# One stage for output projection, first norm and expert layer in a hybrid decoder step

## The chip, the core and the metric

The kernel runs on one core of one Trainium2 chip. The metric is the device time of one execution in microseconds (us); smaller is better. The core has a matrix engine (TensorE, PE in the profile), a vector engine (VectorE, DVE), an activation engine (ScalarE, ACT), a general engine (GpSimd, POOL) and a queue engine (SyncE, SP) that only issues DMAs here. Each engine runs its own list of instructions in order; they meet through semaphores. Three runs of the kernel before gave 3161.84, 3165.94 and 3166.44 us, the median is 3165.94 us.

## The reference, cut to what matters

One decoder layer is computed for 272 prompt positions (16 meta tokens and 256 tokens) and 32 sample positions, width 2048, all in float32. After an input projection and two mixers (a recurrent one and a sparse attention), the part that the change touches is:

```
def finish_layer(x, y_rwkv, y_attn, w_o, ln1_g, ln1_b, peer_wq, peer_subkeys, peer_u, peer_v, ln2_g, ln2_b):
    mix = jnp.concatenate([y_rwkv, y_attn], axis=-1) @ w_o
    x = layer_norm(DN_ALPHA * x + mix, ln1_g, ln1_b)
    return layer_norm(DN_ALPHA * x + peer_ffn(x, peer_wq, peer_subkeys, peer_u, peer_v), ln2_g, ln2_b)
```

`peer_ffn` projects each position to 16 query halves (`x @ peer_wq`), scores them against keys, picks 16 experts of 16384 for each of 8 heads, and sums `gate * gelu(x . u_expert) * v_expert`. The meta positions are dropped after the mixers, so 288 positions remain (256 prompt, 32 sample).

## The kernel before, in words

`build` (line 346) calls a row of phases through `Ctx.phase` (line 114). A phase is one block of code in which all engines run side by side; all engines meet at its end, SP clears the phase's semaphores in a small block of its own, and the next phase starts. So nothing of a later phase, loads included, begins before the phase in front of it is done.

Activations lie transposed: 128 partitions are 128 of the 2048 features, `KT` = 16 blocks of features follow in the free dimension, and positions are innermost. A weight tile is 128 x 2048 floats (1 MB). Products that need more than the reduced `fp32r` precision are split: ACT rounds a tile to `fp32r` ("high"), DVE subtracts ("low"), and `split_product` (line 269) makes three matmuls on lines 272 to 274: high by high, high by low, low by high. A tile is therefore loaded by SP, raised by ACT, lowered by DVE, and then used by PE in 48 matmuls.

After the mixers, five phases follow on lines 385 to 396:

1. `load` "rest" (line 388): the residual, 2.25 MB, from a DRAM buffer into `x_midT`.
2. `split` "mix" (lines 251 to 266): the mixers' output `mixT` into high and low, in four quarters, ACT (line 258) and then DVE (line 264).
3. `project` "out" (line 277): 16 tiles of `w_o`. SP loads four tiles ahead (line 306), ACT raises into two buffers (line 314), DVE lowers the next tile (line 332) ahead of evacuating this one (line 392: `alpha * x + product` into `x_midT`). PE runs 48 matmuls of 288 columns for each tile.
4. `layer_norm` "ln1" (line 179): the mean over features is 16 full-precision matmuls by a matrix of 1/2048 (line 199, two records each), DVE copies and subtracts it in four quarters (lines 210 and 212), ACT squares (line 231), PE sums the squares (line 203), DVE adds epsilon and takes the reciprocal (lines 215 and 216), ACT takes the root (line 234), DVE multiplies 16 blocks by gain and root (line 220) and adds the shift in 16 more (line 224), into `mixT`.
5. `peer_layer` (line 1931): the expert layer, one phase with an order written out by hand. The list `order` puts a query tile of `peer_wq` before every second expert tile as long as there are queries (16), then 128 tiles of `peer_u` ("up", line 2201 and after) and 128 tiles of `peer_v` ("down"). Four weight slots (`SL` = 4) turn in that order: SP loads the next tile of the list once PE is done with the one four places before (line 2073 and after). At the start of the phase, ACT and DVE split the normed activations into `high` and `low` (lines 2286 and 2485), DVE spreads the sample columns (line 2480), PE makes the first query (line 2178: 16 full-precision matmuls of two records each), turns the sample columns (line 2160), and then runs `up(0)`.

The rest of `peer_layer` goes by the number of the tile: `select` on DVE picks the experts in tiles 4 to 35, POOL sends 256 scatters of gates to DRAM (line 2122) as heads are chosen, and gathers the sample rows by indirect DMAs (line 2142); DVE multiplies these in certain tiles (line 2439). DVE's list has these steps between the lowering of tiles (line 2327), so a wait for a gathered row holds up the tile behind it.

Of the kernel before, what the change touches and what calls it, by code (L numbers as in the profile page):

```python
# [19 lines left out]
P = 128  # L20
D = 2048
# [324 lines left out]
def build(nc, a, o):  # L346

    cx = Ctx(nc)
    with ExitStack() as top:
# [35 lines left out]
        with ExitStack() as late:  # L385

            xT = sb("x_midT", [P, KT, NY], stack=late)
            cx.phase(load, "rest", ((xT[:], x_rest[:, :, META:N]),))
            high, low = sb("mix_high", [P, KT, NY], F32R, late), sb("mix_low", [P, KT, NY], F32R, late)
            cx.phase(split, "mix", mixT[:, :, META:N], high, low)  # L390
            cx.phase(project, "out", KT, a["w_o"], high, low,
                    lambda v, c, acc: v.scalar_tensor_tensor(xT[:, c, :], xT[:, c, :], ALPHA, acc,
                                                             ALU.mult, ALU.add))
# [1531 lines left out]
def peer(cx, a, o, xT, whole, ident, gates_d):  # L1925


    cx.phase(peer_layer, a, o, xT, whole, ident, gates_d)


def peer_layer(cx, a, o, xT, whole, ident, gates_d):
# [15 lines left out]
    order = []  # L1947
# [22 lines left out]
    with ExitStack() as st:  # L1970
# [5 lines left out]
        parts = nc.alloc_sbuf_tensor_at("px_parts", [P, S, D], F32, offset=begin)  # L1976
        rows = sb("rows", [P, 2, D])
        xs, acc_s = sb("xs", [P, D]), sb("acc_s", [P, D])
# [3 lines left out]
        fetch = [sb(f"fetch{s}", [P, D]) for s in range(UG)]  # L1982
# [29 lines left out]
        here = begin  # L2012

# [7 lines left out]

        hid = [again(f"hid{s}", [P, NP]) for s in range(HS)]
# [8 lines left out]
        loaded = [cx.sem(f"px_loaded{s}") for s in range(SL)]  # L2031
        keyed = [cx.sem(f"px_keyed{s}") for s in range(4)]
# [18 lines left out]
        with nc.Block() as block:  # L2051
            @block.sync
            def _(sp):
# [18 lines left out]
                for kind, n in order:  # L2072
                    s, turn = slot(kind, n)
                    if turn:
                        before, m = order[at[kind, n] - SL]
                        sp.wait_ge(projected if before == "query" else multiplied, m + 1)
# [35 lines left out]
            def _(pool):  # L2112
                sent = 0
# [37 lines left out]
                pool.wait_ge(multiplied, NK)  # L2151
# [3 lines left out]
            def _(pe):  # L2155
# [15 lines left out]

                def query(c):
# [4 lines left out]
                    for k in range(KT):  # L2177
# [69 lines left out]
            def _(act):  # L2247
                def prepare(u):
                    s, turn = slot("tile", u)
                    act.wait_ge(loaded[s], 16 * (turn + 1))  # L2250
                    if u >= WH:
                        act.wait_ge(multiplied, u - WH + 1)
# [418 lines left out]
```

## Time and profile before

| | us |
|---|---|
| median of 3 runs (3161.84 to 3166.44) | 3165.94 |
| the profiled execution's own time | 3163.14 |
| its span, first to last instruction | 3161.5 |
| PE busy | 2820.4 (89%) |
| DVE busy | 1805.1 (57%) |
| ACT busy | 986.4 (31%) |
| POOL busy | 772.3 (24%) |
| mean granted clock of TensorE | 0.932 |

Rows of a timeline give the start from the span's beginning, the duration, the engine, the line of the code, the operation, and what it writes and reads; `x4` means that four of the kind follow each other and are shown as one, and brackets at the end give the engine's idle time before the row and what ended it. Rows of a table of stretches give busy time and number of instructions of PE, PEld (weight loads), DVE, ACT and POOL in that order, then the granted clock of TensorE as a share of its full 2.4 GHz, the busy share of the DMA engines and GB/s.

### The profile page before, as it was taken

The page shows a single profiled execution, that of the slowest core. Times are in us where ns is not written, and L with a number is a line of the kernel's source. Part 1 is how long each engine was busy: PE and PEld are TensorE (multiplying, and loading weights), DVE is VectorE, ACT ScalarE, POOL GpSimd, SP SyncE. Part 2 cuts the span into 40 slices and gives each one's busy share as a digit, 9 for nine tenths or more (in the row PEclk, how much of TensorE's full clock was granted, in tenths as well). Part 3 has the DMA queues.
Part 4 walks back from the last instruction along what each step waited for, and adds up shares of the span by engine and source line. Part 5 has one row for each costly group of instructions (what it writes and reads, how often), then busy time and mean ns, then how long its engine had stood idle before and what let it go on. Part 6 is the DMA issues. An engine that isn't in the chain of part 4 may idle for free.

```text
span 3161.5 us, 45193 instructions
## 1 busy us (share of the span) xinstructions
PE 2820.4 (89%) x17548; PEld 2427.2 (77%) x17548; DVE 1805.1 (57%) x2598; ACT 986.4 (31%) x1169; POOL 772.3 (24%) x630
## 2 busy tenths in 40 slices
PE   3999984767988999759699997999999999999997
PEld 2999972456666666549599997999999888888886
DVE  3455541198774443233468895555656667666655
ACT  1454530011221111122323233333334434434343
POOL 0100002210000222200018787888840000000000
PEclk7999997687889999879899998999999999999999
DMA  3355434322223555242356666999888888876664
GB/s 124 134 185 182 160 142 126 95 68 63 62 67 107 162 154 155 77 145 105 124 166 173 177 180 173 295 300 289 296 309 304 327 303 306 308 275 249 246 237 176
DMA packets 245312, 594.93 MB, mean 188 GB/s; under 512 B 76345, under 2 KB 180162, under 8 KB 192658
## 3 DMA queue, kind: packets, MB, share of 16 engines
q1 hardware_dynamic: 173874, 484.95, 44.8%
q0 software_dynamic: 54592, 90.41, 10.7%
q10 hardware_dynamic: 16640, 16.78, 1.6%
q8 instruction: 135, 2.21, 0.3%
q14 instruction: 71, 0.58, 0.1%
HBM read 535.05 MB, written 56.97 MB: 187 GB/s over the span
## 4 chain that ended last, share of the span: by engine, by line
PE 31%; POOL 12%; issue 5%; DMA 3%; DVE 1%; ACT 0%; DVEq 0%; POOLq 0%
POOL expert_gates L2122 12%; PE px_bank L272 10%; PE px_bank L274 10%; PE px_bank L273 10%; PE px_bank L2178 1%; DMA expert_gates<-px_chosen,px_spot 1%; POOL px_fetch L2142 1%; DMA px_w<-in_peer_v 1%; DMA px_parts<-sample_parts 0%; DMA px_fetch<-in_peer_rows,px_spots_s 0%; ACT px_wh L2253 0%; DMA px_w<-in_peer_wq 0%; DVE px_rows L2514 0%; DMA px_w<-in_peer_u 0%; DVE px_fetch L2519 0%
## 5 line engine op out<-in xcount | busy, mean ns | idle before, releaser
L2327 DVE TENSOR_TENSOR px_w_r<-px_w,px_wh 128x2048 fp32r<-128x2048 f32 x256 | 585.8, 2291 | 278.9 <-ACT px_wh L2253 278.5
L2253 ACT ACTIVATE px_wh<-px_w 128x2048 fp32r<-128x2048 f32 x256 | 489.8, 1913 | 593.1 <-PE px_bank L274 242.3
L272 PE MATMUL px_bank<-px_high,px_wh 128*128 128x256 f32 x2048 | 584.5, 285 | 24.2 <-DVE px_w_r L2327 24.2
L2122 POOL DMA_INDIRECT expert_gates<-px_chosen,px_spot x256 | 499.0, 1949 | 430.3 <-DVE px_chosen L2401 322.9
L273 PE MATMUL px_bank<-px_low,px_wh 128*128 128x256 f32 x2048 | 581.4, 284 | 0.0
L274 PE MATMUL px_bank<-px_high,px_w_r 128*128 128x256 f32 x2048 | 581.4, 284 | 0.0
L272 PEld LDWEIGHTS px_bank<-px_high,px_wh 128*128 128x128 f32 x2048 | 395.2, 193 | 25.6 <-DVE px_w_r L2327 25.6
L272 PE MATMUL px_bank<-px_wh,px_gh 128*128 128x512 f32 x1024 | 398.5, 389 | 1.2 <-DVE px_gl L2333 1.2
L274 PE MATMUL px_bank<-px_wh,px_gl 128*128 128x512 f32 x1024 | 398.4, 389 | 0.0
L273 PE MATMUL px_bank<-px_w_r,px_gh 128*128 128x512 f32 x1024 | 398.4, 389 | 0.0
L273 PEld LDWEIGHTS px_bank<-px_low,px_wh 128*128 128x128 f32 x2048 | 395.2, 193 | 0.0
L274 PEld LDWEIGHTS px_bank<-px_high,px_w_r 128*128 128x128 f32 x2048 | 395.0, 193 | 0.0
L272 PE MATMUL pj_acc<-mixT_r,pj_wh 128*128 128x304 f32 x784 | 244.4, 312 | 44.0 <-DVE pj_w_r L630 44.0
L274 PE MATMUL pj_acc<-mixT_r,pj_w_r 128*128 128x304 f32 x784 | 241.3, 308 | 0.0
L273 PE MATMUL pj_acc<-x_inT_r,pj_wh 128*128 128x304 f32 x784 | 239.4, 305 | 0.0
L272 PEld LDWEIGHTS px_bank<-px_wh,px_gh 128*128 128x128 f32 x1024 | 192.2, 188 | 41.8 <-DVE px_w_r L2327 1.1
L273 PEld LDWEIGHTS px_bank<-px_w_r,px_gh 128*128 128x128 f32 x1024 | 192.2, 188 | 40.0
L274 PEld LDWEIGHTS px_bank<-px_wh,px_gl 128*128 128x128 f32 x1024 | 192.2, 188 | 39.9
L630 DVE TENSOR_TENSOR pj_w_r<-pj_w,pj_wh 128x2048 fp32r<-128x2048 f32 x49 | 112.7, 2302 | 184.0 <-ACT pj_wh L531 184.0
L272 PEld LDWEIGHTS pj_acc<-mixT_r,pj_wh 128*128 128x128 f32 x784 | 149.9, 191 | 48.6 <-DVE pj_w_r L630 44.7
L2439 DVE SCALAR_TENSOR_TENSOR px_fetch<-px_fetch,px_xs 128x2048 f32<-128x2048 f32 x32 | 73.4, 2292 | 142.2 <-DMA px_fetch<-in_peer_rows,px_spots_s 142.2
L2274 ACT ACTIVATE px_h<-px_bank 128x256 f32<-128x256 f32 x128 | 48.8, 382 | 329.2 <-PE px_bank L274 325.5
(392 smaller groups left out, 4352.1 us busy)
## 6 DMA issues: line engine op xcount, KB each, us to landing
px_w<-in_peer_u SPq DMA_DIRECT2D x128, 1024.0 KB, 5.4
px_w<-in_peer_v SPq DMA_DIRECT2D x128, 1024.0 KB, 4.9
pj_w<-in_w_in SPq DMA_DIRECT2D x49, 1024.0 KB, 4.9
expert_gates<-rh_empty ACTq DMA_DIRECT2D x16, 1024.0 KB, 6.4
at_values<-in_kv_pages POOLq DMA_DIRECT2D x128, 128.0 KB, 2.7
at_pages<-in_kv_pages SPq DMA_DIRECT2D x128, 128.0 KB, 2.2
out_w<-in_w_o SPq DMA_DIRECT2D x16, 1024.0 KB, 4.8
px_w<-in_peer_wq SPq DMA_DIRECT2D x16, 1024.0 KB, 4.9
```

Source lines behind the costliest of these rows:

```text
L272: pe.matmul(out, w_high, high, start=start, stop=False, skip_group_check=True)
L273: pe.matmul(out, w_high, low, start=False, stop=False, skip_group_check=True)
L274: return pe.matmul(out, w_low, high, start=False, stop=stop, skip_group_check=True)
L630: v.tensor_tensor(w_low[c % SL][:], w[c % SL][:], w_high[c % 2][:], ALU.subtract).then_inc(lowered, 1)
L2122: pool.indirect_dma_start(gates_d, bass.IndirectOffsetOnAxis(ap=spot[:, t, z:z + 1], axis=0), chosen[:, 2, t, z:z + 1], None, compute_op=A ...
L2142: pool.indirect_dma_start(fetch[n % UG][:], None, a["peer_rows"] if n < TS else a["peer_v"], bass.IndirectOffsetOnAxis(ap=spots_s[:, r:r + ...
L2178: mm = pe.matmul(acc[:, 0:NY], w[s][:, k * P:k * P + P], xT[:, k, :], start=k == 0, stop=k == KT - 1)
L2253: act.activation(w_high[u % WH][:], w[s][:], ACT.Copy).then_inc(raised, 1)
L2274: act.activation(h[i % HS][:], bank[i % 4][:, 0:NP], ACT.Gelu).then_inc(curved, 1)
L2327: v.tensor_tensor(w_low[s][:], w[s][:], w_high[u % WH][:], ALU.subtract).then_inc(lowered, 1)
L2439: v.scalar_tensor_tensor(to[:], to[:], 1.0, xs[:], ALU.mult, ALU.mult, accum_out=dots[:, r:r + 1]).then_inc(dotted, 1)
```

## The change: what it does

The phases "rest", "mix", "out" and "ln1" are gone; their work moves to the front of `peer_layer`.

- **Weight stream.** The 16 tiles of `w_o` stand ahead of `order`, so they, the queries and the expert tiles pass through the same four slots. Three `w_high` buffers (`WH` = 3) are used where `project` had two. SP issues the first four tiles of `w_o`, then waits for the split of `mixT` (`m_split`) and loads the residual over `mixT`.
- **Split.** ACT raises the first weight tile, then the four quarters of `mixT`; DVE lowers the first quarter, the first weight tile, then the other quarters; PE starts a quarter of the first tile as each quarter is split.
- **Norm sums.** After tile 1, PE takes a rough mean from the first block alone (`first_mean`), DVE makes it a shift (`first_shift`). For every tile DVE evacuates (`empty`) and subtracts the shift (`move_y`), ACT squares the block (`square_y`), and POOL adds block and square to two running sums. After the last tile PE multiplies the two sums and the last block by the matrix of ones (`moments`, four matmuls in place of 32).
- **Rest of the norm.** `deviations` on DVE copies the mean, makes the variance as mean of squares less square of the mean, takes the reciprocal, and subtracts the mean from blocks 0 to 7 in two quarters; POOL subtracts it from blocks 8 to 15 in two quarters. ACT takes the root. DVE multiplies block by block, and ACT adds the shift block by block (`normed_x`).
- **Query 0** starts with block 0 of `normed_x` and takes each block as it comes.

The core of the diff:

```diff
-        with ExitStack() as late:
...
-            cx.phase(load, "rest", ((xT[:], x_rest[:, :, META:N]),))
...
-            cx.phase(split, "mix", mixT[:, :, META:N], high, low)
-            cx.phase(project, "out", KT, a["w_o"], high, low,
...
-            cx.phase(layer_norm, "ln1", xT, ln_gb[:, 1], ones, into=mixT[:, :, META:N])
-        peer(cx, a, o, mixT[:, :, META:N], mixT, ident, gates_d)
+        peer(cx, a, o, mixT[:, :, META:N], mixT, ident, gates_d, x_rest, ones, ln_gb[:, 1])
...
-    order = []
+    order = [("out", c) for c in range(KT)]
...
+                    if kind == "out":
+                        sp.dma_start(w[s][:].rearrange("p (k e) -> p k e", e=P), a["w_o"][n]).then_inc(loaded[s], 16)
+                        if n == 3:
+                            sp.wait_ge(m_split, 4)
+                            sp.dma_start(xT, x_rest[:, :, META:N]).then_inc(rest_in, 16)
+                        continue
...
             def _(pool):
+                for c in range(KT - 1):
+                    pool.wait_ge(moved_y, c + 1)
+                    if c:
+                        pool.wait_ge(summed_y, 2 * c)
+                    for to, x in ((sum_y, xT[:, c, :]), (sum_q, sq[c % 2][:])):
+                        if to is sum_q:
+                            pool.wait_ge(squared_y, c + 1)
+                        if c:
+                            pool.tensor_tensor(to[:], x, to[:], ALU.add).then_inc(summed_y, 1)
+                        else:
+                            pool.tensor_copy(to[:], x).then_inc(summed_y, 1)
+                pool.wait_ge(centered_x, 1)
...
+                for q_ in (2, 3):
+                    four = xT[:, 4 * q_:4 * q_ + 4, :]
+                    pool.tensor_tensor(four, four, norm[:, 1:2, :].to_broadcast([P, 4, NY]), ALU.subtract) \
+                        .then_inc(widened, 1)
...
+                def out(c):
+                    s, _ = slot("out", c)
+                    pe.wait_ge(lowered, c + 1)
+                    if c >= 4:
+                        pe.wait_ge(emptied, c - 3)
+                    for k in range(KT):
+                        if c == 0 and k % 4 == 0:
+                            pe.wait_ge(m_split, k // 4 + 1)
...
+                def first_mean():
+                    pe.wait_ge(emptied, 1)
+                    pe.matmul(bank[5][:, 0:NY], ones[:], xT[:, 0, :], start=True, stop=True).then_inc(shift_made, 1)
...
+                def moments():
+                    pe.wait_ge(summed_y, 2 * KT - 2)
+                    pe.wait_ge(shifted_by, 1)
+                    pe.matmul(bank[5][:, 0:NY], ones[:], sum_y[:], start=True, stop=False)
+                    pe.matmul(bank[6][:, 0:NY], ones[:], sum_q[:], start=True, stop=False)
+                    pe.wait_ge(moved_y, KT)
+                    pe.matmul(bank[5][:, 0:NY], ones[:], xT[:, KT - 1, :], start=False, stop=True).then_inc(meaned, 1)
+                    pe.wait_ge(squared_y, KT)
+                    pe.matmul(bank[6][:, 0:NY], ones[:], sq[(KT - 1) % 2][:], start=False, stop=True).then_inc(meaned, 1)
...
                     for k in range(KT):
+                        if c == 0:
+                            pe.wait_ge(normed_x, k + 1)
                         mm = pe.matmul(acc[:, 0:NY], w[s][:, k * P:k * P + P], xT[:, k, :], start=k == 0, stop=k == KT - 1)
...
+                for c in range(KT):
+                    out(c)
+                    if c == 1:
+                        first_mean()
+                moments()
...
+                prepare(-KT)
+                for z in range(4):
+                    act.activation(m_high[:, 4 * z:4 * z + 4, :], xT[:, 4 * z:4 * z + 4, :], ACT.Copy).then_inc(m_raised, 1)
+                act.activation(stat[:, 0, 7:8], ident[:, 0:1], ACT.Sqrt)
+                for c in range(KT):
+                    if c + 1 < KT:
+                        prepare(c + 1 - KT)
+                    if c:
+                        square_y(c - 1)
+                square_y(KT - 1)
+                act.wait_ge(deviated, 1)
+                act.activation(rs[:, 1, :], rs[:, 0, :], ACT.Sqrt).then_inc(deviated, 1)
+                for k in range(KT):
+                    act.wait_ge(scaled_x, k + 1)
+                    act.activation(xT[:, k, :], xT[:, k, :], ACT.Identity, bias=gb[:, 1, k:k + 1]).then_inc(normed_x, 1)
+                act.wait_ge(normed_x, KT)
...
+                def empty(c):
...
+                    if c == 0:
+                        v.wait_ge(rest_in, 16)
+                    v.scalar_tensor_tensor(x, x, ALPHA, bank[c % 4][:, 0:NY], ALU.mult, ALU.add).then_inc(emptied, 1)
+                def move_y(c):
...
+                    v.tensor_tensor(x, x, norm[:, 0, :], ALU.subtract).then_inc(moved_y, 1)
...
+                def deviations():
...
+                    v.wait_ge(meaned, 1)
+                    v.tensor_copy(norm[:, 1, :], bank[5][:, 0:NY]).then_inc(centered_x, 1)
+                    v.wait_ge(centered_x, 1)
+                    lk(v.tensor_tensor(norm[:, 2, :], norm[:, 1, :], norm[:, 1, :], ALU.mult))
+                    v.wait_ge(meaned, 2)
+                    lk(v.scalar_tensor_tensor(rs[:, 0, :], bank[6][:, 0:NY], LN_EPS, norm[:, 2, :], ALU.add, ALU.subtract))
+                    v.reciprocal(rs[:, 0, :], rs[:, 0, :]).then_inc(deviated, 1)
...
+                    for q_ in range(2):
+                        four = xT[:, 4 * q_:4 * q_ + 4, :]
+                        ins = v.tensor_tensor(four, four, norm[:, 1:2, :].to_broadcast([P, 4, NY]), ALU.subtract)
+                    lk(ins)
+                    v.wait_ge(deviated, 2)
+                    for k in range(KT):
+                        if k in (8, 12):
+                            v.wait_ge(widened, k // 4 - 1)
+                        v.scalar_tensor_tensor(xT[:, k, :], xT[:, k, :], gb[:, 0, k:k + 1], rs[:, 1, :],
+                                               ALU.mult, ALU.mult).then_inc(scaled_x, 1)
...
+                for z in range(4):
+                    v.wait_ge(m_raised, z + 1)
+                    v.tensor_tensor(m_low[:, 4 * z:4 * z + 4, :], xT[:, 4 * z:4 * z + 4, :],
+                                    m_high[:, 4 * z:4 * z + 4, :], ALU.subtract).then_inc(m_split, 1)
+                    if z == 0:
+                        prepare(-KT)
+                for c in range(KT):
+                    if c + 1 < KT:
+                        prepare(c + 1 - KT)
+                    empty(c)
+                    if c == 1:
+                        first_shift()
+                        move_y(0)
+                    if c:
+                        move_y(c)
+                deviations()
+                v.wait_ge(normed_x, KT)
```

In `out`, `square_y` and the lines left out, waits keep the buffers free of overlap; `prepare` on ACT now waits for PE to be three tiles behind. The new phase has 15 more semaphores than `peer_layer` had.

## Rows read from the trace of the kernel before

**Rows 1.** Table of stretches: output projection, norm to first expert matmul, first expert tiles.

```profile
1387.00:1491.60 104.60, 104.55 (x768) 104.31 (x768) 41.20 (x31) 26.85 (x15) 0.00 (x0) 0.98 0.36 130
1491.60:1549.04 57.44, 30.80 (x112) 23.19 (x113) 31.47 (x64) 13.84 (x14) 0.00 (x0) 0.76 0.22 78
1549.04:1642.00 92.96, 92.96 (x651) 86.23 (x650) 46.25 (x116) 28.88 (x35) 0.00 (x0) 1.00 0.49 170
```

**Rows 2.** Timeline, residual load to the first evacuation of the output projection, all engines.

```profile
1359.89 0.58 SPq L166 DMA_DIRECT2D x_midT<-x_rest  x1
...
1370.25 4.32 ACT L258 ACTIVATE mix_high<-mixT 128x1152 fp32r<-128x1152 f32 x4 [15.38 <-PEq L120]
1371.45 5.16 DVE L264 TENSOR_TENSOR mix_low<-mixT,mix_high 128x1152 fp32r<-128x1152 f32 x4 [15.05 <-ACT mix_high L258]
1377.77 88.69 SPq L306 DMA_DIRECT2D out_w<-in_w_o  x16
1382.72 1.91 ACT L314 ACTIVATE out_wh<-out_w 128x2048 fp32r<-128x2048 f32 x1 [8.14 <-DMA out_w<-in_w_o]
1384.66 4.69 DVE L332 TENSOR_TENSOR out_w_r<-out_w,out_wh 128x2048 fp32r<-128x2048 f32 x2 [8.05 <-ACT out_wh L314]
1387.01 0.61 PE L272 MATMUL out_acc<-mix_high,out_wh 128*128 128x288 f32 x1 [35.22 <-DVE out_w_r L332]
...
1395.72 0.45 DVE L392 SCALAR_TENSOR_TENSOR x_midT<-x_midT,out_acc 128x288 f32 x1 [6.38 <-PE out_acc L274]
```

**Rows 3.** Timeline, last evacuation to the first expert matmul, all engines.

```profile
1491.59 0.45 DVE L392 SCALAR_TENSOR_TENSOR x_midT<-x_midT,out_acc 128x288 f32<-128x288 f32 x1 [5.94 <-PE out_acc L274]
...
1506.51 9.72 PE L203 MATMUL ln_var<-ln_sq,ones 128*128 128x288 f32 x32 [3.14 <-ACT ln_sq L231]
...
1516.76 1.95 DVE L216 RECIPROCAL ln_rs<-ln_rs 128x288 f32<-128x288 f32 x1
...
1519.22 6.96 DVE L220 SCALAR_TENSOR_TENSOR x_midT<-x_midT,ln_gb,ln_rs 128x288 f32<-128x288 f32 x16 [0.51 <-ACT ln_rs L234]
...
1532.26 0.34 SPq L2078 DMA_DIRECT2D px_w<-in_peer_wq  x1
...
1532.52 2.19 DVE L2480 COPY px_acc_s<-mixT 128x128 f32<-128x128 f32 x16
...
1534.63 4.62 DVE L2485 TENSOR_TENSOR px_low<-mixT,px_high 128x1024 fp32r<-128x1024 f32 x4
...
1537.63 9.91 PE L2178 MATMUL px_bank<-mixT,px_w 128*128 128x288 f32 x32 [21.41 <-DMA px_w<-in_peer_wq]
...
1549.04 0.36 PE L272 MATMUL px_bank<-px_high,px_wh 128*128 128x256 f32 x1
```

**Rows 4.** The residual's tile: time from issue of its load to landing.

```profile
DMA to landing us min/median/max: 9.3/9.3/9.3
```

**Rows 5.** Chain of waits, second query (start, duration).

```profile
1561.22 7.76 PE px_bank L2178 x32
```

**Rows 6.** Table of stretches, the variance matmuls of the norm.

```profile
1506.50:1516.30 9.80, 9.72 (x32) 7.06 (x32) 2.60 (x4) 3.49 (x3) 0.00 (x0) 0.83 0.00 0
```

**Rows 7.** Timeline, elementwise work of POOL and DVE beside each other, in earlier phases.

```profile
86.27 4.94 DVE L630 TENSOR_TENSOR pj_w_r<-pj_w,pj_wh 128x2048 fp32r<-128x2048 f32 x2 [11.05 <-ACT pj_wh L531]
...
86.69 2.36 POOL L619 TENSOR_TENSOR pj_df<-pj_raw 128x272 f32<-128x272 f32 x1 [19.04 <-ACT pj_last L589]
...
98.72 0.64 POOL L619 TENSOR_TENSOR pj_df<-pj_raw 128x272 f32<-128x272 f32 x1 [7.26 <-ACT pj_last L589]
...
755.58 1.89 POOL L1110 TENSOR_TENSOR rh_bx<-rh_rows,rh_seqmask 128x1024 f32<-128x1024 f32 x1 [50.23 <-DMA rh_rows<-rw_rows]
...
755.86 1.77 DVE L1872 TENSOR_SCALAR at_prob<-at_prob,at_stat 128x272 f32<-128x272 f32 x1
...
806.47 0.50 DVE L1872 TENSOR_SCALAR at_prob<-at_prob,at_stat 128x272 f32<-128x272 f32 x1
```

**Rows 8.** Waits of PE from 1642 to 2165 us: total, times, longest.

```profile
PE px_bank L272 <- DVE px_w_r L2327: 24.2, 7, 12.6
```

More of the change, by code:

```diff
@@ L1976, in peer_layer @@
         parts = nc.alloc_sbuf_tensor_at("px_parts", [P, S, D], F32, offset=begin)
+        begin = -(-nc.sbuf_base // 32) * 32
         rows = sb("rows", [P, 2, D])
+        fetch = [sb(f"fetch{s}", [P, D]) for s in range(UG)]
+        m_high, m_low = (nc.alloc_sbuf_tensor_at(f"px_m_{x}", [P, KT, NY], F32R, offset=begin + z * KT * NY * 4)
+                         for z, x in enumerate(("high", "low")))
+        assert nc.sbuf_base >= begin + 2 * KT * NY * 4
         xs, acc_s = sb("xs", [P, D]), sb("acc_s", [P, D])
@@ L2012, in peer_layer @@
         here = begin
+        norm = sb("norm", [P, 3, NY])
         def again(name, shape, dt=F32):
@@ L2020, in again @@
             return t
+        here = begin + 4 * 4 * P
+        sq = [again(f"sq{s}", [P, NY]) for s in range(2)]
+        sum_y, sum_q = again("sum_y", [P, NY]), again("sum_q", [P, NY])
+        rs = again("rs", [P, 2, NY])
+        here = begin
         hid = [again(f"hid{s}", [P, NP]) for s in range(HS)]
@@ L2192, in up @@
                     s, _ = slot("tile", i)
-                    pe.wait_ge(lowered, i + 1)
+                    pe.wait_ge(lowered, KT + i + 1)
                     if i >= 4:
@@ L2206, in down @@
                     s, _ = slot("tile", u)
-                    pe.wait_ge(lowered, u + 1)
+                    pe.wait_ge(lowered, KT + u + 1)
                     pe.wait_ge(g_lowered, j + 1)
@@ L2248, in prepare @@
                 def prepare(u):
-                    s, turn = slot("tile", u)
+                    r = KT + u
+                    s, turn = slot("tile", u) if u >= 0 else slot("out", r)
                     act.wait_ge(loaded[s], 16 * (turn + 1))
-                    if u >= WH:
-                        act.wait_ge(multiplied, u - WH + 1)
-                    act.activation(w_high[u % WH][:], w[s][:], ACT.Copy).then_inc(raised, 1)
+                    if r >= WH:
+                        act.wait_ge(multiplied, r - WH + 1)
+                    act.activation(w_high[r % WH][:], w[s][:], ACT.Copy).then_inc(raised, 1)
                     if u >= NK:
@@ L2268, in keep_rows, with square_y @@
                     act.activation(rows[:, t, c * 512:c * 512 + 512], bank[7][:], ACT.Copy, scale=ALPHA).then_inc(rowed, 1)
+                def square_y(c):
+                    act.wait_ge(moved_y, c + 1)
+                    if c >= 2:
+                        act.wait_ge(summed_y, 2 * (c - 2) + 2)
+                    act.activation(sq[c % 2][:], xT[:, c, :], ACT.Square).then_inc(squared_y, 1)
                 def curve(i):
-                    act.wait_ge(multiplied, i + 1)
+                    act.wait_ge(multiplied, KT + i + 1)
                     if i >= HS:
@@ L2320, in prepare @@
                 def prepare(u):
-                    s, _ = slot("tile", u)
+                    r = KT + u
+                    s, _ = slot("tile", u) if u >= 0 else slot("out", r)
                     if u >= NK:
```

47 lines of the change are left out of this document (32 added, 15 removed).

## The prediction

> **What bounds the kernel now.** I read the table of stretches first. PE is busy for 104.55 of 104.60 us in the output projection and for all of 92.96 us once the expert tiles run; between them lie 57.44 us with 30.80 us of PE work at a granted clock of 0.76 [rows 1]. So the edges are open and the middle is not: PE sets the pace inside both product stages, and a serial chain through the other engines sets it in front of the first and between the two. The timelines of these edges come next. In front, the residual's load (1359.89), the split (1370.25), the first weight load (1377.77) and the first matmul (1387.01) follow each other [rows 2]. Between, the norm, a weight load (issued at 1532.26, its query at 1537.63) and the split stand in one line [rows 3]. Both are parts of the chain that I expect to set the end, since PE has no gap from 1549.04 to 1642 [rows 1] and what follows is numbered by tiles; the one later place where PE waits is 24.2 us in seven waits [rows 8].
>
> **The front.** The first DMA of the stage stays where the residual's was, at 1359.89, and is now a weight tile. In the old order the tile reached ACT 4.95 us after issue (1377.77 to 1382.72), and raising took 1.91 [rows 2]. So it is raised at 1366.75. Then ACT raises the first quarter of the mix (4.32 for four, 1.08 each) and DVE lowers it (5.16 for four, 1.29 each) [rows 2]: 1369.2. DVE then lowers the weight tile, 2.35, half of 4.69 [rows 2]; with hops 1371.7, and PE begins, against 1387.01 [rows 2]: **15.3 us gained**. The other quarters (1.29 each) finish before PE needs them, since a quarter of the first tile is over 2 us of PE: the first tile took 8.7 us (1387.01 to 1395.72) [rows 2].
>
> **The projection.** The other 15 tiles took 1395.72 to 1491.59, 6.39 each [rows 2, 3]. In the new list DVE does 2.35 + 0.45 + 0.46 (the move, taken as an evacuation) a tile, ACT 1.91 + 0.45 (the square, taken likewise), POOL two sums of 0.68 (0.64 for 272 columns, scaled to 288) [rows 2, 3, 7]. Each engine fits in 6.39. The order matters more. ACT's raise of tile c+2 stands behind the square of block c-1, done 1.5 us after PE finishes tile c-1; raised 1.9 later, lowered by DVE behind the evacuation and move of tile c, 3.3 us after PE finishes tile c, when PE needs it 6.39 after: 3.1 us to spare. That spare covers POOL's sums even if they block DVE (1.36 a tile). So the pace stays. Three additions: `first_mean` costs two records, 7.76/16 = 0.5 [rows 5]. DVE's wait for the residual has the lowering of tile 2 behind it: the residual is issued when the fourth quarter is split, 1371.7 + 3 x 1.29 = 1375.6, lands 9.3 later [rows 4] at 1384.9, then evacuation and lowering end at 1387.8. PE is ready at 1371.7 + 8.7 + 6.39 + 0.5 = 1387.3: 0.5 lost. The same engines' round through shift, move, square, raise and lower for tile 3 ends at 1394.1 where PE is done with tile 2 at 1394.2; I add 0.5 for it. **1.5 us lost**, between 0 (residual early) and 4 (it lands 3 us later beside weights).
>
> **From the last tile to the expert tiles.** Call PE's end of the last output tile T. Before, T was 1491.55 and `up(0)` began at 1549.04: 57.5 us [rows 3]. After, in the new chain: evacuation 0.5; move 1.0; two records for the last block 1.6; mean copied 2.1 (0.46 each for small DVE steps, as the evacuation); its square and the variance 3.1; reciprocal 1.95 [rows 3], 5.1. DVE then subtracts two quarters, 2.6, beside POOL's two, which begin at about 2.1 and last 1.89 x 1152/1024 = 2.13 each [rows 7]. These two engines hold each other up in both directions [rows 7]: POOL's 0.64 us sum took 2.36 when DVE's lowering had begun at 86.27, and DVE's 0.50 us scaling took 1.77 when POOL's product had begun at 755.58. With the small square in the same contest POOL ends at 6.9, and DVE's quarters start there: 9.5. If they did not hold each other up it would be 7.7. The multiplies take 6.96, 16.5, and ACT's last shift some 0.45 behind them, 17.0 [rows 3]; the 16 shifts that DVE did are gone from the chain. DVE's spread takes 2.19 and the lowering of the activations 4.62 [rows 3]; `up(0)`'s own lowering 2.35; with memsets and hops 26.6. ACT's work in these (high quarters, two raised tiles, the sample rows) lies beside it: quarters by 17.0 + 4 x 1.08 = 21.3, two tiles of 1.91 by 25.1 [rows 2], and the first sample row, which alone is needed, within a microsecond of that. So `up(0)` begins at T + 26.6, **30.9 us gained**.
>
> Four loads for the first query and expert tiles are issued as PE releases slots in the last tiles of the projection, so their landing costs nothing; what hides them is 26.6 us of norm. Without that cover the first would cost what it did, 1532.26 to 1537.63. Query 0 starts with the first normed block at T + 10.5 and takes 9.9 as before [rows 3], then the samples are turned, and it ends at T + 22; begun after all blocks it would end at T + 29, two us past DVE. That is all the block-wise start is worth.
>
> **The page's rule against it.** The two holds above are in [rows 7], and the sum has them. The Trainium skill (Perfetto Trace Analysis, Optimizing Scalar/DVE Operations) warns that offloading between VectorE and GpSimd may not help, as they share an SBUF read port. By that rule, with which this trace agrees, the two quarters given to POOL save DVE 0.8 us instead of 2.6 and the sum is 42.3; without it the sum would be 44.1.
>
> **Clock.** The 32 records that took 7.76 us at full clock [rows 5] took 9.72 after 3.14 us of idleness [rows 3], at a mean granted clock of 0.83 [rows 6], a mixture of 1.2 and 2.4 GHz; so a start after a gap costs 2.0. Before, `up(0)` ran behind the query without a gap. Now PE stands still from T + 22 to T + 26.6: **2.0 us lost**, between 0 and 2.1. The gap in front of query 0 costs nothing, DVE is later.
>
> **The end.** SP clears 15 more semaphores after the last store. A whole step between phases, clearing two, took 1.2 us after the split (1376.6 to 1377.77) [rows 2]; clearing alone is a part of that, so I take **0.4 us**, between 0 and 1.2. The unrolled matmuls (the old ones were a loop) cost nothing: the straight-line expert tiles show PE without a gap [rows 1].
>
> **Sum.** -15.3 + 1.5 - 30.9 + 2.0 + 0.4 is -42.3, from 3163.14 to 3120.8. The profiled execution lies 2.8 below the median of the runs shown and inside them; by the median it would be 3123.6. I give 3122.
>
> **Rivals.**
> - *A tile of the projection costs PE a wait.* If DVE loses more than its 3.1 us a tile to POOL and to the longer list, PE waits; at 0.7 us a tile (one POOL sum) 11 us: 3133. For it: the two holds [rows 7]. Against: the order above.
> - *The loads are not early, or the norm is not taken block by block.* If the first query tile lands only after the norm, or a block waits for the whole, some 5 us of the old line come back: 3127. For it: slots free only as PE finishes the tiles four places before. Against: those finish 26 us earlier.
> - *Given back at the gathers.* POOL's scatters and gathers feed DVE, which feeds PE, and PE waited 24.2 us there [rows 8]. If their contest with DVE falls worse after the shift and the waits double: 3146. Against: scatters and DVE's steps are numbered by tiles and move with PE.
> - *Slower.* If a tile's preparation starts only behind the evacuation of the one before, the tile becomes a serial round: 0.45 + 0.46 + 0.45 + 1.91 + 2.35 + 6.39 = 12.0, which is 5.6 a tile, 84 over 15: 3206. It decides from 2.8 us a tile, a pace over 9.2. For it: the ACT list puts raises behind squares and these behind DVE. Against: three raised buffers let PE be two tiles behind.
>
> **Numbers.** Forecast 0.69, own range 3112 to 3131 (no contest or clock loss below; late residual, a second cold start and 3 us of run spread above). 3127: 0.10; 3133: 0.08; 3146: 0.08; slower 0.03; no change 0.02. The range 3110 to 3140 holds the first three less their tails. A change under 0.2% (6 us) is about what a measurement of this kernel can't tell from none. Faster 0.95, same 0.02, slower 0.03.
>
> **What would show it.** Right: first output matmul near 1371.7; 16 tiles in some 106 us with PE idle only at tile 2 or 3; DVE's quarters longer than 1.3 each or started late beside POOL; `up(0)` some 27 us after the last output matmul, behind DVE's lowering, at the lower clock; everything from there to the end the same length (1549.04 to the end, 1614 us). Wrong: PE idle before each output tile; `up(0)` behind a DMA or an activation; PE's waits behind gathers over 30 us; a longer tail.

## The result, and the profile after

The changed kernel took 3114.49 us (median of 4 runs, 3107.15 to 3119.91) where the kernel before took 3163.89 (4 runs, 3159.83 to 3166.44): a ratio of 0.9844, 95% interval 0.9816 to 0.9871, 49.4 us less. The forecast was 3122 in a range of 3110 to 3140. Measured once more later, the same two kernels gave 3119.13 (6 runs) and 3157.29 (11 runs, 3141.29 to 3172.19), a ratio of 0.9882 (0.9849 to 0.9914). The two intervals overlap between 0.985 and 0.987; why one repetition shows 49 us and the other 38 is the first question below.

The page of the changed kernel, first lines (span, then busy time, share and instructions):

```profile
span 3108.2 us, 44967 instructions
## 1 busy us (share of the span) xinstructions
PE 2798.7 (90%) x17494; PEld 2412.2 (78%) x17494; DVE 1807.9 (58%) x2598; ACT 993.0 (32%) x1198; POOL 828.6 (27%) x662
```

The timeline of the changed kernel from the mixers' last write to the first output matmul answers to [rows 2]:

```profile
1347.82 0.47 DVE L1138 TENSOR_TENSOR mixT<-rh_y,rh_post 128x304 f32<-128x304 f32 x1
1351.77 1.99 SPq L2083 DMA_DIRECT2D px_w<-in_w_o  x4
1356.61 1.91 ACT L2317 ACTIVATE px_wh<-px_w 128x2048 fp32r<-128x2048 f32 x1 [9.85 <-DMA px_w<-in_w_o]
1358.43 4.30 ACT L2357 ACTIVATE px_m_high<-mixT 128x1152 fp32r<-128x1152 f32 x4
1359.61 1.36 DVE L2606 TENSOR_TENSOR px_m_low<-mixT,px_m_high 128x1152 fp32r<-128x1152 f32 x1 [11.32 <-ACT px_m_high L2357]
1360.88 2.28 DVE L2414 TENSOR_TENSOR px_w_r<-px_w,px_wh 128x2048 fp32r<-128x2048 f32 x1
1363.22 0.61 PE L272 MATMUL px_bank<-px_m_high,px_wh 128*128 128x288 f32 x1 [19.55 <-DVE px_w_r L2414]
```

The line to see is 1351.77: where the old kernel issued the residual's load alone, four weight tiles are issued, and ACT raises the first of them 4.8 us later, ahead of the split. From the first DMA to the first matmul are 11.45 us, where [rows 2] had 27.1. But that DMA itself stands 8.1 us earlier than the old kernel's, behind code that nobody changed.

The timeline from the last evacuation to the end of the first expert tile (the row of 1504.47, the next work in PE's list, marks it) answers to [rows 3]:

```profile
1469.00 0.46 DVE L2510 SCALAR_TENSOR_TENSOR mixT<-mixT,px_bank 128x288 f32<-128x288 f32 x1 [5.45 <-PE px_bank L274]
1469.49 0.46 DVE L2516 TENSOR_TENSOR mixT<-mixT,px_norm 128x288 f32<-128x288 f32 x1
...
1470.79 0.46 DVE L2526 COPY px_norm<-px_bank 128x288 f32<-128x288 f32 x1 [0.85 <-PE px_bank L2224]
...
1471.33 6.57 POOL L2140 TENSOR_TENSOR mixT<-mixT,px_norm 128x1152 f32<-128x1152 f32 x2 [6.13 <-DVE px_norm L2526]
...
1472.27 1.95 DVE L2531 RECIPROCAL px_rs<-px_rs 128x288 f32<-128x288 f32 x1
1474.14 4.97 DVE L2536 TENSOR_TENSOR mixT<-mixT,px_norm 128x1152 f32<-128x1152 f32 x2
...
1479.15 6.96 DVE L2542 SCALAR_TENSOR_TENSOR mixT<-mixT,ln_gb,px_rs 128x288 f32<-128x288 f32 x16
1479.70 6.97 ACT L2369 ACTIVATE mixT<-mixT,ln_gb 128x288 f32<-128x288 f32 x16 [5.00 <-DVE mixT L2542]
1480.38 10.30 PE L2236 MATMUL px_bank<-mixT,px_w 128*128 128x288 f32 x32 [9.15 <-ACT mixT L2369]
...
1489.03 4.62 DVE L2629 TENSOR_TENSOR px_low<-mixT,px_high 128x1024 fp32r<-128x1024 f32 x4
...
1495.95 0.55 PE L272 MATMUL px_bank<-px_high,px_wh 128*128 128x256 f32 x1 [3.53 <-DVE px_w_r L2414]
1504.47 0.60 PE L2198 MATMUL px_bank<-ident,mixT 128*128 128x128 f32 x4
```

PE ended the last output tile at 1468.96 (DVE's evacuation starts 0.04 behind it), so the first expert matmul comes 27.0 us later, where [rows 3] had 57.5. It waits for DVE's lowering, after 3.53 us of idleness, and its tile takes 8.5 us. The norm is a chain on DVE from 1469.00 to the last lowering: apart from 0.85 us of waiting for the mean and 0.65 us for ACT's last shift, every microsecond of it is DVE at work or DVE held up in its two subtractions (4.97 for what takes 2.6 alone).

### The profile page after: what moved, and what is told of

Same layout as the page of the kernel before. It is cut to its first block, busy times and chain, and to the rows that moved or that the text cites. A ratio compares the mean times of both kernels' runs of the same rounds, so it can differ in the third digit from the quotient of the medians.

```text
span 3108.2 us, 44967 instructions
## 1 busy us (share of the span) xinstructions
PE 2798.7 (90%) x17494; PEld 2412.2 (78%) x17494; DVE 1807.9 (58%) x2598; ACT 993.0 (32%) x1198; POOL 828.6 (27%) x662
## 4 chain that ended last, share of the span: by engine, by line
PE 32%; POOL 15%; issue 5%; DMA 2%; DVE 2%; ACT 0%; DVEq 0%; POOLq 0%
POOL expert_gates L2151 14%; PE px_bank L272 10%; PE px_bank L274 10%; PE px_bank L273 10%; POOL px_fetch L2171 1%; PE px_bank L2236 1%; DMA expert_gates<-px_chosen,px_spot 1%; DMA px_parts<-sample_parts 0%; DVE px_w_r L2414 0%; DMA px_fetch<-in_peer_rows,px_spots_s 0%; DMA px_w<-in_peer_v 0%; ACT mixT L2369 0%; ACT px_wh L2317 0%; DVE px_rows L2658 0%; DMA px_w<-in_peer_u 0%
## 5 line engine op out<-in xcount | busy, mean ns | idle before, releaser
L2414 DVE TENSOR_TENSOR px_w_r<-px_w,px_wh 128x2048 fp32r<-128x2048 f32 x272 | 622.3, 2290 | 276.5 <-ACT px_wh L2317 275.6
L2317 ACT ACTIVATE px_wh<-px_w 128x2048 fp32r<-128x2048 f32 x272 | 519.9, 1912 | 589.7 <-PE px_bank L274 265.1
```

What stands on the lines that cost most here:

```text
L2317: act.activation(w_high[r % WH][:], w[s][:], ACT.Copy).then_inc(raised, 1)
L2414: v.tensor_tensor(w_low[s][:], w[s][:], w_high[r % WH][:], ALU.subtract).then_inc(lowered, 1)
```

## Where the spread of the runs is, and what the change is worth

I cut each profile at two points: the end of the mixers' last write, and the end of the first expert tile. Everything that the change touches lies between them, but for the semaphores cleared at the very end. The first stretch of each table begins at 436.00 us, near the end of the input projection, the same in all tables. Tables of stretches (length, then busy time of PE, PEld, DVE, ACT, POOL, granted clock, DMA share, GB/s), first the kernel before:

```profile
436.00:1356.40 920.40, 737.07 (x4393) 522.76 (x4391) 472.77 (x778) 139.34 (x321) 148.58 (x216) 0.84 0.36 102
1356.40:1554.88 198.48, 141.19 (x929) 133.34 (x929) 80.67 (x100) 52.34 (x38) 0.00 (x0) 0.84 0.34 124
1554.88:3161.50 1606.62, 1565.17 (x9778) 1417.59 (x9776) 1038.69 (x1457) 605.13 (x568) 591.30 (x326) 0.99 0.76 253
```

The changed kernel:

```profile
436.00:1348.29 912.29, 727.55 (x4384) 515.54 (x4383) 473.26 (x778) 138.11 (x320) 148.68 (x216) 0.85 0.37 102
1348.29:1504.47 156.18, 128.50 (x875) 124.36 (x875) 84.01 (x100) 60.59 (x67) 55.16 (x32) 0.88 0.44 158
1504.47:3108.20 1603.73, 1566.39 (x9778) 1419.12 (x9776) 1037.64 (x1456) 603.54 (x567) 592.44 (x326) 0.99 0.76 254
```

The middle part is 42.3 us shorter. The kernel before was then run and profiled once more, unchanged:

> The kernel before, unchanged. In the profiles at hand the mixers' last write of their output ends at 1356.4 us before and at 1348.3 us after the change, though the code up to there is the same. Theory A (run to run spread of the mixers' phase): this run's last write lies anywhere between about 1346 and 1360, and not always near 1356.4. Rival B (the new program makes the earlier phases faster): it lies within 1 us of 1356.4 here, and within 1 us of 1348.3 in every run of a kernel made from the changed one. Both: from that write on the stages have the lengths of the first profile: 30.6 us to the first output matmul, 104.5 us of output projection, 57.5 us to the first expert matmul, 1612.5 us from there to the end of the span.

It took 3147.96 us. Its table of stretches:

```profile
436.00:1340.65 904.65, 721.39 (x4395) 511.94 (x4393) 472.67 (x778) 139.82 (x321) 148.66 (x216) 0.86 0.37 104
1340.65:1538.50 197.85, 140.97 (x929) 133.12 (x930) 80.72 (x101) 52.39 (x38) 0.00 (x0) 0.84 0.34 124
1538.50:3146.30 1607.80, 1566.94 (x9778) 1419.31 (x9776) 1040.52 (x1457) 604.57 (x568) 588.93 (x326) 0.99 0.76 253
```

The same program ended its mixers 15.8 us earlier than in its first profile; the middle part moved by 0.6. So rival B is out: the changed program has no faster mixers, the mixers' phase wanders. The first rows of the two tables show where: PE stood idle for 183.3 us in both, and its busy time for the same matmuls differs by 15.7 us (737.07 against 721.39), at a granted clock of 0.84 against 0.86. So in this pair the phase is longer by what its matmuls took longer, at a lower clock; why the clock was lower in one run is not shown, and in the other profiles the idle time moves too (179 to 189 us).

The changed kernel, unchanged, in more runs:

> The changed kernel, unchanged. Theory A (the change saves what its stages show, about 45 us from the mixers' last write to the end, and the rest of the spread is the mixers' phase and the gathers): 3163 less 45 gives 3112 to 3122 for the median, ratio to the kernel before 0.985 to 0.988; from the mixers' last write to the end of the span 1757 to 1764 us, where the kernel before has 1805 to 1806. Rival B (the change also shortens the mixers' phase): median under 3110, ratio under 0.983.

Measured: 3119.13, ratio 0.9882 as told. Its table of stretches:

```profile
436.00:1347.43 911.43, 732.25 (x4384) 520.04 (x4382) 473.95 (x778) 138.10 (x320) 148.72 (x216) 0.84 0.37 102
1347.43:1502.65 155.22, 126.60 (x874) 122.14 (x875) 83.97 (x101) 60.58 (x67) 55.15 (x32) 0.90 0.45 159
1502.65:3116.20 1613.55, 1567.19 (x9778) 1418.66 (x9776) 1037.54 (x1456) 604.86 (x567) 599.96 (x326) 0.99 0.76 252
```

The median lies where theory A had it, but from the mixers' last write to the end were 1768.8 us, over the 1757 to 1764 that I had written. The excess is in the last part, 1613.55, which PE spent with nearly the same 1567 us of work; its waits for DVE's lowering there, the waits of [rows 8], came to 26.7 us where the first profile of the changed kernel had 18.6 and those of the kernel before 24.2 and 22.0. So two parts outside the change wander, the mixers by some 16 us and the expert stage by some 10, and the middle part doesn't: 198.48 and 197.85 before, 156.18 and 155.22 after. **The change is worth 42.5 us** (means of the two), and 49 or 38 is that plus what the rest happened to do.

## Experiments: which part of the change brings what

Lengths are from PE's end of the last output tile, called T, unless told otherwise; the changed kernel has its first expert matmul at 27.0 and the end of that tile at 35.5. In its second profile the start is 27.0 again and the end 34.25, so starts can be compared to about 0.1 us, ends only to about 1.3. Each experiment is one profile, unless more runs are told.

**The norm's sums after the last tile.** Running sums, squares and moves were taken out of the projection, and the old norm put behind it in the same stage:

```diff
-                    pe.matmul(bank[5][:, 0:NY], ones[:], sum_y[:], start=True, stop=False)
-                    pe.matmul(bank[6][:, 0:NY], ones[:], sum_q[:], start=True, stop=False)
+                    for k in range(KT):
+                        mm = pe.matmul(bank[5][:, 0:NY], ones[:], xT[:, k, :], start=k == 0, stop=k == KT - 1)
...
+                        mm = pe.matmul(bank[6][:, 0:NY], ones[:], sq_all[:, k, :], start=k == 0, stop=k == KT - 1)
```

> One stage as in the change, but the norm's sums are made after the last tile as in the old norm: 32 matmul records for the mean, four subtractions on DVE, squares on ACT, 32 records for the squares. Theory A (the sums made tile by tile are a main part of the gain): from the last output matmul to the first expert matmul 10.3 us to the end of the mean (matmuls with a start at the low clock, no phase step) + 15.8 us to the root as in the old timeline + 16.8 us from the first multiply as in the changed kernel = 43 us, where the changed kernel has 27.0; the output projection 0.5 us shorter. Rival B (merging the phases was what counted and the sums hide behind other waits): 32 us or less.

It took 3126.37 us. Timeline, the last evacuation, the first multiply and the first expert matmul:

```profile
1471.91 0.45 DVE L2491 SCALAR_TENSOR_TENSOR mixT<-mixT,px_bank 128x288 f32<-128x288 f32 x1 [5.95 <-PE px_bank L274]
...
1496.29 6.95 DVE L2518 SCALAR_TENSOR_TENSOR mixT<-mixT,ln_gb,px_rs 128x288 f32<-128x288 f32 x16 [0.51 <-ACT px_rs L2347]
...
1513.09 0.55 PE L272 MATMUL px_bank<-px_high,px_wh 128*128 128x256 f32 x1 [4.13 <-DVE px_w_r L2395]
```

The first expert matmul comes at 1513.09 - 1471.87 = 41.2: theory A, with 1.8 less, since the mean's matmuls followed the last tile after 0.55 us and took 8.03 us, not the 9.7 that I had carried over from a start after a gap. So of the 30.5 us gained between T and the first expert matmul, 14.2 come from making the sums tile by tile, and the other 16.3 from the one stage (weights loaded ahead, two phase steps, shifts on ACT), which no run took apart further.

**Weights behind the split.**

```diff
+                        if n == 0:
+                            sp.wait_ge(m_split, 4)
```

(and the order on ACT and DVE: four quarters first, then the tile.)

> The changed kernel, but the first weight tile is loaded only when the mixers' output is split (ACT and DVE split first, then raise and lower the tile); the residual's load stays off the path. From the mixers' last write to the first output matmul the changed kernel has 14.9 us, the old one 30.6. Theory A (of the 15.7 us gained, some 4 come from loading weights ahead of the split and the rest from the residual's load of 9.3 us and two phase steps being off the path): 19 us. Rival B (the weights loaded ahead are the gain): 27 us or more.

It took 3122.26 us. Timeline, mixers' last write to first output matmul:

```profile
1353.45 0.47 DVE L1138 TENSOR_TENSOR mixT<-rh_y,rh_post 128x304 f32<-128x304 f32 x1
1363.81 1.99 SPq L2085 DMA_DIRECT2D px_w<-in_w_o  x4
1373.10 0.61 PE L272 MATMUL px_bank<-px_m_high,px_wh 128*128 128x288 f32 x1 [23.79 <-DVE px_w_r L2415]
```

From 1353.92 to 1373.10 are 19.2 us: theory A. Of the front's 15.7 us, 4.3 come from the early weights and 11.4 from the residual's load and the phase steps.

**Query 0 on whole activations.**

```diff
-                    for k in range(KT):
-                        if c == 0:
-                            pe.wait_ge(normed_x, k + 1)
+                    if c == 0:
+                        pe.wait_ge(normed_x, KT)
+                    for k in range(KT):
```

> The changed kernel, but query 0 waits for all 16 normed blocks. The first expert matmul now starts 27.0 us after the last output matmul and the first expert tile takes 8.5 us, at half the granted clock at first. Theory A (the block-wise start only moves PE's gap in front of the first expert tile, and the gap costs clock): the first expert matmul starts at 29.2, behind the query and the turned samples without a gap, the tile takes 6.2 at the full clock, and it ends at 35.4 us, where the changed kernel's ends at 35.5. Rival B (the clock does not depend on the gap): starts at 29.2, takes 8.5 and ends at 37.7.

It took 3113.33 us. T was 1473.48, the first expert matmul came at 1503.23 (29.75) without a gap, and the tile's end at 1509.06, 35.6. The granted clock of that tile, here and in the changed kernel:

```profile
1503.20:1509.06 5.86, 5.86 (x51) 5.86 (x50) 0.62 (x1) 3.62 (x6) 0.00 (x0) 1.00 0.42 168
```

```profile
1495.95:1504.47 8.52, 8.52 (x49) 8.52 (x49) 4.32 (x2) 3.58 (x4) 0.00 (x0) 0.64 0.00 0
```

Theory A: the tile takes 5.83 us (1503.23 to 1509.06) at the full 2.4 GHz where PE comes from work, and 8.52 at a mixture of 2.4 and 1.2 GHz where it comes from 3.5 us of idleness. So the block-wise start of query 0, one of the parts of the change, brings little by itself: of the 2.75 us that it saves in front it pays back 2.7 in the clock in the first profile of the changed kernel and 1.4 in the second (34.25 against 35.6). It is worth 0.1 to 1.3 us.

**PE kept at work in the gap.** 16 matmuls that nobody reads, behind the turned samples:

```diff
+                            for _ in range(16):
+                                pe.matmul(bank[6][:, 0:P], ident[:], ident[:], start=True, stop=True)
```

> The changed kernel with 16 more full-precision matmuls of 128 columns, whose product nobody reads, between the turned samples and the first expert tile, 3.5 us, the length of PE's gap. Theory A (the gap is what lowers the clock): the first expert matmul starts at 27.0 us after the last output matmul as before, the tile takes 6.2 in place of 8.5 and ends at 33.2. Rival B (the first tile is slow for another cause, its operands or its place): it ends at 35.5 or later.

It took 3117.6 us. T was 1470.52; the tile's end came at 1503.53, 33.0 (theory A, 33.2), and its stretch ran at the full clock:

```profile
1497.60:1503.50 5.90, 5.90 (x52) 5.90 (x51) 4.23 (x2) 3.48 (x4) 0.00 (x0) 1.00 0.01 3
```

The first expert matmul came at 27.2 (27.0 without these matmuls), and the tile took 5.83. Same operands, same place, another clock: the gap is what lowers it.

**POOL's half of the subtractions.** First a quarter moved to DVE (`for q_ in (3,)` on POOL, `range(3)` on DVE):

> The changed kernel, but DVE subtracts the mean from three quarters and POOL from one. In the changed kernel POOL's two subtractions take 6.57 us together and DVE's two 4.97, and the first multiply starts 10.2 us after the last output matmul. Theory A (an operation of POOL and one of DVE with two inputs in the core's memory run one after the other): POOL's quarter is done before DVE begins, DVE's three take 1.3 each, the first multiply starts at 9.1, the first expert matmul at 25.9 in place of 27.0. Rival B (DVE's subtractions are slow by themselves here, 2.5 each): DVE's three take 7.5, the first multiply starts at 12.7.

It took 3115.39 us. Timeline:

```profile
1475.28 2.88 POOL L2140 TENSOR_TENSOR mixT<-mixT,px_norm 128x1152 f32<-128x1152 f32 x1 [6.13 <-DVE px_norm L2526]
...
1478.09 3.83 DVE L2536 TENSOR_TENSOR mixT<-mixT,px_norm 128x1152 f32<-128x1152 f32 x3
1481.95 6.96 DVE L2542 SCALAR_TENSOR_TENSOR mixT<-mixT,ln_gb,px_rs 128x288 f32<-128x288 f32 x16
```

Three quarters on DVE, alone, take 3.83 us; two beside POOL took 4.97. The first multiply starts at 9.0, the first expert matmul at 25.8: theory A to 0.1 us. Then all of the norm's POOL work on DVE, sums too:

```diff
+                    for z in (0, 1) if c == 2 else (c - 1,) if c > 2 else ():
+                        sum_one(z)
                     empty(c)
...
-                    for q_ in range(2):
+                    for q_ in range(4):
```

> The changed kernel with POOL's part of the norm on DVE: the 30 running sums between the lowering and the evacuation of a tile, and all four subtractions of the mean. Theory A (DVE has the time inside the projection, and at its end POOL's half only stands in DVE's way): the projection keeps its 105.7 us from first matmul to last, DVE's four subtractions take 5.2 from 5.2 us after the last output matmul, the first multiply starts at 10.4 where the changed kernel has 10.2, and the first expert matmul at 27.2 in place of 27.0. Rival B (POOL's sums are what lets DVE keep up): PE waits in the projection, which takes 107 us or more, or the first expert matmul starts later than 28.5.

It took 3104.36 us. Timeline:

```profile
1465.86 5.09 DVE L2529 TENSOR_TENSOR mixT<-mixT,px_norm 128x1152 f32<-128x1152 f32 x4
1470.99 6.96 DVE L2533 SCALAR_TENSOR_TENSOR mixT<-mixT,ln_gb,px_rs 128x288 f32<-128x288 f32 x16
```

T was 1460.68: the projection took 105.9 us, the first multiply starts at 10.3 and the first expert matmul (1487.80) at 27.1. Theory A: POOL's 30 sums and two subtractions together are worth 0.1 us. The sums show why. Minimum, median and maximum of a duration in ns, of POOL's sums of the blocks and of DVE's lowerings in the changed kernel:

```profile
L2132 POOL TENSOR_TENSOR px_sum_y<-mixT,px_sum_y x14: 809/2786/2796, 1381.8 to 1463.6; 128x288 f32<-128x288 f32 x14
```

```profile
L2414 DVE TENSOR_TENSOR px_w_r<-px_w,px_wh x272: 2281/2291/2295, 1360.9 to 3076.6; 128x2048 fp32r<-128x2048 f32 x136
```

POOL's sum takes 0.81 us when DVE is idle and 2.79 when it begins just behind a lowering; not one of 272 lowerings took over 2.295. In the projection POOL is the one that is held up, which costs nothing: with the sum of squares behind it (0.80, median) it needs 3.6 of the 6.4 us of a tile.

**A shorter chain.** The first expert tile raised and lowered before the last evacuation, where ACT and DVE stood idle (`prepare(c + 1 - KT)` also for the last `c`, and no `prepare(0)` behind the norm):

> The changed kernel, but the first expert weight tile is raised and lowered before the last evacuation of the output projection, where ACT and DVE wait for PE, and not behind the norm. Both: the first expert matmul starts when DVE has lowered the activations, 24.7 us after the last output matmul in place of 27.0, and PE's gap in front of it shrinks from 3.5 to 1.3 us. Theory A (in the changed kernel the granted clock fell late in the gap, its mean over the gap was 0.91): the tile runs at the full clock, 6.2 us, and ends at 31. Rival B (any gap lowers the clock): 8.5 us, it ends at 33.2.

It took 3116.48 us. Timeline, PE:

```profile
1503.31 0.39 PE L272 MATMUL px_bank<-px_high,px_wh 128*128 128x256 f32 x1 [0.91 <-DVE px_low L2626]
1509.16 0.60 PE L2198 MATMUL px_bank<-ident,mixT 128*128 128x128 f32 x4
```

T was 1478.57: start at 24.7, end at 30.6, theory A. The lowering off the chain saves 2.3 us, and the clock that the shorter gap keeps up 2.7 more (1.4 against the second profile of the changed kernel). With the single POOL quarter added:

> The changed kernel with both edits: the first expert tile raised and lowered before the last evacuation, and three quarters subtracted by DVE, one by POOL. Alone the one ended the first expert tile 30.6 us after the last output matmul, the other 33.15, the changed kernel 35.5. Theory A (both shorten the same chain on DVE, so they add, and the clock stays up since PE's gap is under 1.5 us): start at 23.6, 5.9 us, end at 29.5, some 6 us less than the changed kernel; the median of the runs 3 to 9 us under the changed kernel's, which 5 runs of each can hardly tell from none. Rival B (the gap lowers the clock again, or query and sample turning end last): end at 31.5 or later.

Measured 3115.4 us (6 runs, ratio to the kernel before 0.9861, 0.9827 to 0.9895). T was 1478.91; start at 23.6 as expected, but after a gap of 1.96 us, longer than I had counted, and the tile took 7.35 at a lowered clock: end at 30.95, between the two theories. The query of `lower_early`, then the query and the first expert matmul of this run:

```profile
1489.99 10.67 PE L2236 MATMUL px_bank<-mixT,px_w 128*128 128x288 f32 x32 [9.14 <-ACT mixT L2368]
```

```profile
1489.18 9.62 PE L2236 MATMUL px_bank<-mixT,px_w 128*128 128x288 f32 x32 [8.00 <-ACT mixT L2368]
1502.51 0.43 PE L272 MATMUL px_bank<-px_high,px_wh 128*128 128x256 f32 x1 [1.96 <-DVE px_low L2626]
```

So the two edits do not add. Query and lowering both begin 1.15 us sooner behind T, which alone would leave the gap as it was; but the query also took 9.62 us in place of 10.67, so PE was done sooner and the gap came back. With 8 matmuls in it that nobody reads:

> The kernel with both edits (first expert tile lowered early, three quarters on DVE), and 8 matmuls of 128 columns that nobody reads in PE's gap of 2 us in front of the first expert tile. With both edits alone that tile started at 23.6 us after the last output matmul and took 7.35. Theory A (what is left is the clock after the gap): starts at 23.6, takes 5.9, ends at 29.5 in place of 35.5 in the changed kernel. Rival B: it ends at 30.9 or later. By whole times neither can be told from the changed kernel, whose stages in front of and behind these differ by 10 us from run to run.

Measured 3108.18 us (4 runs, 3101.45 to 3112.66; ratio to the kernel before 0.9829, 0.9785 to 0.9874). Timeline, PE:

```profile
1501.04 0.38 PE L272 MATMUL px_bank<-px_high,px_wh 128*128 128x256 f32 x1 [0.28 <-DVE px_low L2628]
...
1506.89 0.60 PE L2198 MATMUL px_bank<-ident,mixT 128*128 128x128 f32 x4
```

T was 1477.44: start at 23.6, end at 29.45, theory A. By its stages this version is some 5 to 6 us shorter than the changed kernel; its interval overlaps the changed kernel's two, so whole times do not show it.

## Why the prediction was right

- **Front**, 15.3 us gained: from the mixers' last write to the first output matmul 30.6 (second profile 30.3) before, 14.9 (14.8) after, so 15.7 (15.5). Each step fell within 0.4 us of the working. Right.
- **Projection**, 1.5 us lost: 104.5 before, 1468.96 - 1363.22 = 105.7 after, 1.2 lost; 104.4 and 106.15, so 1.7 lost, in the second profiles. The residual landed 9.4 us after its issue, and DVE waited 7.2 us for it with the lowering of tile 2 behind it. The first row is this wait in the first profile, the second is PE's first matmul of tile 2 in the second profile:

```profile
1376.39 0.45 DVE L2510 SCALAR_TENSOR_TENSOR mixT<-mixT,px_bank 128x288 f32<-128x288 f32 x1 [7.22 <-DMA mixT<-x_rest]
```

```profile
1378.54 0.40 PE L272 MATMUL px_bank<-px_m_high,px_wh 128*128 128x288 f32 x1 [1.30 <-DVE px_w_r L2414]
```

In the second profile PE waited 1.30 us at tile 2, where the working had 0.5. In the first it waited nowhere, because its first two tiles had run longer (15.46 us at a granted clock of 0.81, against 14.35 at 0.89), so that it came to tile 2 just as the lowering ended. The cause that the working named is right; that 1.2 comes so near to 1.5 is partly luck. Tile 3 cost nothing in either, its lowering ended 0.6 us before PE needed it.
- **Last tile to the expert tiles**, 30.9 us gained: 57.5 before, 27.0 after, 30.5 gained. The contest of POOL and DVE, taken from [rows 7], put DVE's subtractions at their end at 9.5; they ended at 10.15. POOL's two took 6.57, with DVE's quarter let in between them, and the working had a quarter of POOL 0.3 us too short each time (2.89 for the first, with DVE's square in it, where it had 2.13 and 0.46). Without the contest the working had 7.7. So the two quarters on POOL save DVE 0.1 us (10.3 in the run with no work on POOL), not the 0.8 of the working.
- **Clock**, 2.0 us lost: the tile took 5.84 before (1549.04 to 1554.88) and 8.52 after, 2.7 lost, which is over the bound of 2.1; 7.25 in the second profile, 1.4 lost. Right in kind, and shown by the kept-at-work run; the size varies from run to run.
- **Sum to the end of the first expert tile**: 42.7 by these four terms as forecast; 42.3 in the first pair of profiles, 42.6 in the second.
- **The end**, 0.4: what the execution's time has beyond the span went from 1.64 to 2.14 us, and from 1.66 to 2.39 in the second profiles.
- **The rest unchanged**: 1606.6 and 1607.8 before, 1603.7 and 1613.6 after. No run shows a change, but the spread is larger than I had allowed, and the mixers' phase, of which the prediction said nothing, moved by 8 us between the two profiles. The 7.5 us by which 3122 missed the first measurement are of that kind; the second median, 3119.1, is 2.9 off.
- **The step that was wrong**: "begun after all blocks it would end at T + 29, two us past DVE. That is all the block-wise start is worth." It is worth 0.1 to 1.3 us (35.6 against 35.5 and 34.25 at the end of the tile): a query that ends later leaves no gap, so the loss that I had booked under the clock is the price of the block-wise start. Two terms that I worked out one by one belong together.
- **The rivals**: none of them came. In the projection PE waited only at tile 2, for 0.5 to 1.3 us in six of the eleven profiles of the changed kernel and its variants and not at all in the others; its first expert matmul waited for DVE's lowering and not for a load; and its waits for lowerings at the gathers stayed between 16 and 27 us in all runs, those of the kernel before included. The serial round of the slower rival was near only for tile 3.

## What to carry to other kernels

Where two busy stages are joined by a serial chain, add up the chain by engine, put the loads and sums of the second stage into the idle slots of the first, and expect the gain to be the sum of what left the chain; a stage by stage comparison shows it to a microsecond where whole times of one program lie up to 31 us apart. An engine that is given half of a job may get it at the price of the engine that it helps: check in the trace whether their operations run beside each other or in turn. Price an idle gap in front of TensorE work together with the edit that makes it, since closing the gap gave back its length and the clock here (2.3 and 1.4 to 2.7 us), and filling it the clock alone (1.2 to 2.5).

## What the runs showed that I had not expected

- The mixers' phase, the same code in all kernels here, ended anywhere between 1339.8 and 1358.3 us in the profiles, and the kernel's whole times before ran from 3141 to 3172; three runs within 5 us of each other had suggested far less. The 0.2% (6 us) that the prediction took as the limit of a measurement was too small for single runs.
- The first expert tile took 5.85 us after 0.9 us of idleness, 7.25 to 7.35 after gaps of 2.0, 2.9 and 3.3 us, and 8.2 to 8.5 after 3.5 to 4.1 us; already 2 us of idleness cost 1.5 us.
- When POOL and DVE wanted to work at once in the projection it was POOL, which began second, that waited (2.79 us for 0.81), while in the subtractions at its end the two engines went in turn and both were longer.
